# Splitting the first weight sum, its high part and its low part into halves where two seven-product units meet

## What is computed

```python
x = x + 0.5 * swiglu(rmsnorm(x, ffn1_norm[i]), ffn1_w_gu[i], ffn1_w_down[i])
...
x = x + m
x = x + 0.5 * swiglu(rmsnorm(x, ffn2_norm[i]), ffn2_w_gu[i], ffn2_w_down[i])
...
def swiglu(x, w_gu, w_down):
    gate, up = jnp.split(x @ w_gu, 2, axis=-1)
    return (jax.nn.silu(gate) * up) @ w_down
```

## Time and profile before

| what | value |
|---|---|
| median of 3 runs | 2016.92 us (2016.15 to 2017.0) |
| the profiled execution | 2016.95 us |
| its span | 2015.2 us |
| mean granted TensorE clock | 0.999 of full speed |
| TensorE busy | 1987.3 us, 99% |
| VectorE busy | 1680.8 us, 83% |
| ScalarE busy | 1242.4 us, 62% |

### The profile page before, as it was taken

How to read it: one execution, slowest core, us unless ns; L and a number is a source line. 1 busy time by engine, 2 the same in 40 slices (tenths; PEclk the granted TensorE clock), 3 DMA queues, 4 the chain that set the end, 5 groups by cost and what they waited for, 6 DMA issues and landing times.

```text
span 2015.2 us, 25299 instructions
## 1 busy us (share of the span) xinstructions
PE 1987.3 (99%) x10203; PEld 1684.0 (84%) x10203; DVE 1680.8 (83%) x1569; ACT 1242.4 (62%) x1317; POOL 189.3 (9%) x181
## 2 busy tenths in 40 slices
PE   7999999999999999999999999999999999999998
PEld 6888998888888889988888878988888888998877
DVE  7997568997999789969987997779988997568996
ACT  6565576665666566646665665446665665576664
POOL 2000001010000014411001010001001000001010
PEclk9999999999999999999999999999999999999999
DMA  9896535996897484368995996758986896535992
GB/s 278 274 268 214 181 105 141 277 258 222 231 270 230 146 271 131 126 230 222 277 272 162 277 253 191 209 186 232 286 257 175 268 267 216 176 105 144 275 261 103
DMA packets 250632, 436.65 MB, mean 217 GB/s; under 512 B 10924, under 2 KB 93188, under 8 KB 250004
## 3 DMA queue, kind: packets, MB, share of 16 engines
q1 hardware_dynamic: 215732, 363.34, 53.1%
q0 software_dynamic: 34496, 71.39, 19.7%
q10 hardware_dynamic: 288, 0.31, 0.0%
HBM read 433.92 MB, written 1.08 MB: 216 GB/s over the span
## 4 chain that ended last, share of the span: by engine, by line
PE 72%; DVE 14%; ACT 7%; issue 4%; DMA 2%; DVEq 0%; ACTq 0%; SPq 0%; POOLq 0%; POOL 0%
PE bank L1620 36%; PE bank L1761 23%; PE bank L1626 7%; DVE w_lo L1126 6%; ACT w_hi L744 6%; PE bank L1795 2%; DVE stage L1264 2%; DVE arena L1487 2%; DVE arena L1264 1%; DMA arena<-in_ffn_w_gu 1%; PE bank L1653 1%; PE bank L1935 1%; PE bank L1966 1%; PE bank L1948 0%; DMA stage<-in_ssd_w_in 0%
## 5 line engine op out<-in xcount | busy, mean ns | idle before, releaser
L1126 DVE TENSOR_TENSOR w_lo<-stage,w_hi 128x2048 fp32r<-128x2048 f32 (+1 forms) x245 | 562.3, 2298 | 85.1 <-ACT w_hi L744 82.5
L744 ACT ACTIVATE w_hi<-stage 128x2048 fp32r<-128x2048 f32 (+1 forms) x245 | 463.0, 1893 | 220.6 <-PE bank L1620 109.8
L1126 DVE TENSOR_TENSOR w_lo<-arena,w_hi 128x2048 fp32r<-128x2048 f32 (+1 forms) x199 | 450.3, 2267 | 81.6 <-ACT w_hi L744 80.0
L744 ACT ACTIVATE w_hi<-arena 128x2048 fp32r<-128x2048 f32 (+1 forms) x199 | 376.7, 1897 | 184.8 <-PE bank L1620 87.3
L1620 PE MATMUL bank<-w_hi,mt_hi 128*128 128x512 f32 x928 | 366.5, 395 | 0.4 <-DVE mt_lo L1373 0.4
L1620 PE MATMUL bank<-w_lo,mt_hi 128*128 128x512 f32 x928 | 361.4, 389 | 0.0
L1620 PE MATMUL bank<-w_hi,mt_lo 128*128 128x512 f32 x928 | 360.8, 390 | 0.0
L1761 PE MATMUL bank<-w_hi,mt_hi 128*128 128x512 f32 x512 | 205.2, 401 | 7.9 <-DVE w_lo L1126 7.8
L1620 PEld LDWEIGHTS bank<-w_hi,mt_lo 128*128 128x128 f32 x928 | 174.2, 188 | 36.9
L1626 PE MATMUL bank<-xt_hi,w_hi 128*128 128x256 f32 x704 | 203.4, 290 | 1.6 <-DVE arena L1487 1.1
L1620 PEld LDWEIGHTS bank<-w_hi,mt_hi 128*128 128x128 f32 x928 | 174.3, 188 | 35.4 <-DVE mt_lo L1373 0.8
(11 more groups left out here) (219 smaller groups left out, 2957.3 us busy)
## 6 DMA issues: line engine op xcount, KB each, us to landing
arena<-in_ffn_w_gu SPq DMA_DIRECT2D x82, 1024.0 KB, 5.9
stage<-in_ffn_w_gu SPq DMA_DIRECT2D x78, 1024.0 KB, 5.3
stage<-in_ffn_w_down SPq DMA_DIRECT2D x100, 512.0 KB, 5.0
arena<-in_ffn_w_down SPq DMA_DIRECT2D x76, 512.0 KB, 5.5
arena<-in_ffn_w_gu POOLq DMA_DIRECT2D x35, 1024.0 KB, 9.0
stage<-in_ffn_w_gu POOLq DMA_DIRECT2D x29, 1024.0 KB, 10.1
arena<-in_ffn_w_gu SPq DMA_DIRECT2D x20, 512.0 KB, 6.9
arena<-in_sb_w_qkv SPq DMA_DIRECT2D x16, 512.0 KB, 4.7
```

Of the source, the lines that this page charges most:

```text
L744: act.activation(w_hi[q][:, 0:c], stage[s][:, 0:c], ACT.Copy).then_inc(hi_done, 1)
L1126: dve.tensor_tensor(w_lo[q][:, 0:c], stage[s][:, 0:c], w_hi[q][:, 0:c].bitcast(F32), ALU.subtract).then_inc(lo_done, 1)
```

## The change

At the 24 places where two S units meet, the sum for A1, its high part and its low part are each done in two halves of 1024 columns (`HALF`), with new semaphores `sum_half`, `hi_half` and `lo_half`. On VectorE the low part's two halves now follow right behind the sum's, and `second_gate` comes behind them. TensorE's A1 waits for the first half before its first matmul and for the whole block before its seventh. The sum takes one more wait, for the low part of B11, whose block it overwrites.

```diff
--- before.py
+++ after.py
@@ -98,6 +98,12 @@
     return order + waiting + [(u, f"D{j}") for j in range(down_parts(u))], turned
 
 
+def junctions_to(f, u):
+
+    return f * sum(adjacent(v) for v in range(len(UNITS))) + sum(adjacent(v) for v in range(u + 1))
+
+
+HALF = (slice(0, 1024), slice(1024, 2048))
 FFN_ORDER, TURNED_AFTER = ffn_order()
 N_UNITS, N_SUMS = len(UNITS), UNITS.count("S")
 HOME = {"A1": "B11", "A2": "B11", "A3": "B12", "A4": "B21"}
@@ -429,6 +435,7 @@
         row_done = sem("row_done")
         xn_done, xn_act, xn_gained = sem("xn_done"), sem("xn_act"), sem("xn_gained")
         first_hi, first_lo = sem("first_hi"), sem("first_lo")
+        sum_half, hi_half, lo_half = sem("sum_half"), sem("hi_half"), sem("lo_half")
         xt_ps = sem("xt_ps")
         xg_done = sem("xg_done")
         xt_hi_done = sem("xt_hi_done")
@@ -731,6 +738,13 @@
                 p = max(r for r in range(n_phases) if base[r] <= n)
                 u, name = FFN_ORDER[n - base[p]] if PHASES[p][0] == "ffn" else (0, None)
                 sums = sums_before(nth("ffn", p), u)
+                if name == "A1" and adjacent(u):
+                    act.wait_ge(block_used, n - SPLIT_SLOTS + 1)
+                    act.wait_ge(sum_half, junctions_to(nth("ffn", p), u))
+                    act.activation(w_hi[q][:, HALF[0]], stage[s][:, HALF[0]], ACT.Copy).then_inc(hi_half, 1)
+                    act.wait_ge(w_summed, len(SUM_STEP) * sums + SUM_STEP[name])
+                    act.activation(w_hi[q][:, HALF[1]], stage[s][:, HALF[1]], ACT.Copy).then_inc(hi_done, 1)
+                    return
                 if name in SUM_STEP:
                     act.wait_ge(w_summed, len(SUM_STEP) * sums + SUM_STEP[name])
                 elif name == "A2":
@@ -1263,6 +1277,26 @@
                         to, a, b = w("B21"), w("B21"), w("B11")
                     dve.tensor_tensor(to, a, b, ALU.add).then_inc(w_summed, 1)
 
+                def weight_sum_by_halves(u):
+
+                    w = lambda b: stage[home[p, u, b][0]]
+                    dve.wait_ge(lo_done, b0 + FFN_ORDER.index((u, "B11")) + 1)
+                    dve.wait_ge(stage_in[home[p, u, "B12"][0]], home[p, u, "B12"][1])
+                    dve.tensor_tensor(w("B11")[:, HALF[0]], w("B12")[:, HALF[0]], w("B11")[:, HALF[0]],
+                                      ALU.add).then_inc(sum_half, 1)
+                    dve.tensor_tensor(w("B11")[:, HALF[1]], w("B12")[:, HALF[1]], w("B11")[:, HALF[1]],
+                                      ALU.add).then_inc(w_summed, 1)
+
+                def split_by_halves(u, n):
+
+                    s, q = slot_of[n], n % SPLIT_SLOTS
+                    dve.wait_ge(hi_half, junctions_to(f, u))
+                    dve.tensor_tensor(w_lo[q][:, HALF[0]], stage[s][:, HALF[0]], w_hi[q][:, HALF[0]].bitcast(F32),
+                                      ALU.subtract).then_inc(lo_half, 1)
+                    dve.wait_ge(hi_done, n + 1)
+                    dve.tensor_tensor(w_lo[q][:, HALF[1]], stage[s][:, HALF[1]], w_hi[q][:, HALF[1]].bitcast(F32),
+                                      ALU.subtract).then_inc(lo_done, 1)
+
                 def x_sums():
                     for i, (a, b, op) in enumerate(((xg[:, 1, :], xg[:, 3, :], ALU.subtract),
                                                     (x_sum[:, 0, :], xg[:, 0, :], ALU.subtract),
@@ -1319,12 +1353,15 @@
                         released(*FFN_ORDER[i - 1], i - 1)
                     if i == 1 and N_SUMS:
                         x_sums()
-                    if i + 2 <= len(FFN_ORDER) and (i == 0 or FFN_ORDER[i - 1] != (N_UNITS - 1, "A2")):
+                    if i + 2 < len(FFN_ORDER) and FFN_ORDER[i + 2][1] == "A1" and adjacent(FFN_ORDER[i + 2][0]):
+                        pass
+                    elif i + 2 <= len(FFN_ORDER) and (i == 0 or FFN_ORDER[i - 1] != (N_UNITS - 1, "A2")):
                         split(b0 + i + 2)
                     if i + 1 < len(FFN_ORDER):
                         u, name = FFN_ORDER[i + 1]
                         if name == "B11" and adjacent(u):
-                            weight_sum(u, "A1")
+                            weight_sum_by_halves(u)
+                            split_by_halves(u, b0 + i + 3)
                             second_gate(u - 1)
                         elif i >= 1 and FFN_ORDER[i - 1][1] == "A4" and adjacent(FFN_ORDER[i - 1][0] + 1):
                             hidden_summed(FFN_ORDER[i - 1][0], 1)
@@ -1753,9 +1790,11 @@
                                               start=kh == 0 and k == 0, stop=kh == 1 and k == 3)
                     mm.then_inc(block_used, 1)
 
-                def product(n, out_, x_, start, stop):
+                def product(n, out_, x_, start, stop, whole_from=None):
 
                     for k in range(4):
+                        if k == whole_from:
+                            block_in(n)
                         x, w = x_(k), w_pair(n, 512 * k, 512)
                         for a, b in PASSES:
                             mm = pe.matmul(out_[:, :], x[a], w[b], start=start and k == 0 and (a, b) == (0, 0),
@@ -1798,7 +1837,9 @@
 
                 for i, (u, name) in enumerate(FFN_ORDER):
                     n = b0 + i
-                    if n > 0:
+                    if name == "A1" and adjacent(u):
+                        pe.wait_ge(lo_half, junctions_to(f, u))
+                    elif n > 0:
                         block_in(n)
                     if n == 0:
                         opening_block()
@@ -1820,7 +1861,7 @@
                         product(n, bank[4], x_part(0, 0), True, True)
                     elif name == "A1":
                         pe.wait_ge(xs_lo_done, 4 * (f + 1))
-                        product(n, bank[5], x_sum_part(0), True, True)
+                        product(n, bank[5], x_sum_part(0), True, True, 2 if adjacent(u) else None)
                     elif name == "B22":
                         pe.wait_ge(part_copied, 3 * sums_before(f, u) + 2)
                         product(n, bank[5], x_sum_part(3), False, True)
```

## The result

| | before | after |
|---|---|---|
| median | 2016.96 us (4 runs, 2016.15 to 2017.28) | 2030.46 us (4 runs, 2030.39 to 2030.61) |
| ratio | | 1.0066, 95% interval 1.0054 to 1.0079 |
| span of the profiled run | 2015.2 us | 2028.6 us |
| mean granted clock | 0.999 | 1.0 |

The change makes the kernel slower by 13.5 us, 0.66%. Slower was forecast, with 2024.7 us; the time lies 1 us above the range, which ended at 2029.5.

What follows compares the result with a forecast made beforehand. TensorE, 99% busy, was taken as the bound, gaining or losing only by holes in its matmul stream. B22 starting 0.32 to 0.33 us later at 24 junctions adds 7.8 to 2016.9: 2024.7 us, range 2020 to 2029.5.

Steps and rivals of the forecast that it cites:

- The hole before A1: TensorE's wait for A1's low part at 24 junctions: 0.49 us each, forecast to go, with 1.44 to spare.
- a larger hole: TensorE before B22: forecast wait of about 0.9 us, with the start at 108.85 instead of a possible 107.93.
- the lateness of B22: TensorE's B22 at each junction: forecast to start at 108.85 against 108.53, 0.32 us later.
- the four halves: VectorE, two sum and two low-part halves at 1.13 each plus some waiting: 4.59 us before the second partial sum.
- not a third hole, but near one: TensorE's first down block after B22: its low part forecast in time by less than 0.1 us, so no wait.
- The hidden low part: VectorE's low part for the first down block: first bank forecast done at 111.51, block due to start at 111.65.
- such a restart at A1: TensorE's first matmul after the wait ahead of A1: 0.11 us extra, counted in the 0.60 per junction.
- the case of two holes: Rival: the down block's low part is late too, or halves cost 1.22; shift 0.5 to 0.7, 2029 to 2033, chance 0.13.
- TensorE's finer waits: TensorE's separate waits for A1's first half and, ahead of the seventh matmul, the second: costed at nothing.
- The earlier start of A2's load: POOL queue's second accumulating load, released by A1's low part: goes out 1.9 us earlier, costed at nothing.
- the hole that simply goes: Rival: ScalarE's lateness is swallowed, each junction gains 0.60, 14.4 us in all, 2002.5 us; chance 0.08.
- the 0.60: TensorE at A1, per junction: 0.49 us of waiting plus 0.11 for the first matmul after; 14.4 us over 24.

## Why the prediction was right and wrong

**Right: the mechanism.** The hole before A1 goes (0.49 in the row, 0 after), the second partial sum slips to 4.69 after the sum (4.59 forecast), the SiLU to 5.41 (5.30), B22's high part to 6.51 (6.39), the copy of A1's product to 10.12 (9.99), and a larger hole opens before B22, ended by that copy. Two runs show that this chain is the cause, each by one move: with the partial sum earlier, or the SiLU further back, the loss turns into a gain. The move without the halves has the same loss in large, and the copy moved out of the queue gives back its own length.

**Wrong: the size, 0.56 per junction instead of 0.32 to 0.33.** Two terms of the sum were too small.

The first is the lateness of B22. From A1's start to B22's I had 4.62; it measured 4.74, which is 24 times 0.12, 2.9 us. The step that was mis-sized is the one of the four halves: 4.69 from the sum to the second partial sum, where the sum had 4.59. From there to B22's start the way is as forecast, 6.15 (104.13 to 110.28, against 102.70 to 108.85), and A1's start lies 6.12 behind the sum's, as forecast. Within the halves it went wrong where ScalarE stands between them: the sum's first half took 0.09 to reach ScalarE (100.66 to 100.75), where I had taken 0.03 from a row with a whole block, so the low part started 2.41 after the sum instead of 2.33; the rest is a half that follows at 1.14, not 1.13. The mean over the junctions adds 0.02 to this one's 4.72.

The second is the step that I called "not a third hole, but near one". The hidden low part was forecast in time by less than 0.1 (my own figures, 111.51 and 111.65, are 0.14 apart), with nothing charged for the way to TensorE. Its first bank was ready at 112.99, and TensorE started the down block at 113.13; the distance is 0.15 at all 24 junctions, so the margin was used up. Undisturbed it would have started at 112.88 + 0.23 = 113.11. That delay is nearly nothing, but the first matmul after it took 0.31 to the next instead of 0.23. I had charged such a restart at A1 in the row before (0.11), and forgot it here: 0.02 and 0.08 at 24 places are 2.4 us. Forecast 7.8, plus 2.9 and 2.4, makes 13.1 of the 13.4 us by which the span grew.

The range took its upper end from the case of two holes, a rival that I put at 2029 to 2033 with a chance of 0.13. This is where the time fell: both holes, but with halves at 1.14 rather than at their full 1.22.

**What was costed at nothing.** TensorE's finer waits: nothing, as shown by their own run. The earlier start of A2's load: nothing in the changed kernel. But my rival of the hole that simply goes, 2002.5 us, was worked out with the same silence on the loads, and there it was wrong: at the junctions the 0.60 was had, and about half of it was lost again behind them, because loads that were hardly waited for at the old pace were waited for at the new one. I had looked at the issue times of the loads and not at how late they land.

**Breaking up instructions.** The Trainium skill (Perfetto Trace Analysis, Optimizing Scalar/DVE Operations) says that breaking up instructions on engines that cause bubbles may let work finish sooner. The run with the halves alone bears it out, by 7.3 us. In the changed kernel the finished work was not the work that was needed next.

## What to carry to other kernels

When work on one engine is moved ahead, look at what it is moved past, who reads that, and above all what else stands in the reader's in-order queue: 0.68 us of work that came 2.5 later cost 0.5 at each of 24 places, only because four instructions for someone else stood behind its reader. Count the slack of each consumer before and after: the gain of the first hole shortens the slack of the second by the same amount. And when an experiment gains half of the hole's worth, look for the transfer that was hidden until then; cutting it in half in both kernels tells quickly whether it is the one.

## What was not expected of the hardware

The distance from the end of one engine's instruction to the start of the one that waits for it on another engine differs from place to place, and hardly at all from junction to junction. From VectorE to ScalarE it was 0.03 for a whole block before the change and 0.09 for the sum's first half (at all junctions but the first). To TensorE it was 0.06 from A1's low part before the change, 0.14 to 0.15 from the copy of A1's product, and 0.15 from the hidden low part in the changed kernel. Each is small; on a chain with several such steps at 24 places they were a part of the miss.

A stop of TensorE costs more than its length. The first matmul of the down block started 0.00 to 0.05 late at the 24 junctions of the changed kernel, and at each of them the next one followed after 0.31 instead of 0.23. In the kernel with whole blocks in the new order, with a hole of 2.1 us at each junction, the granted clock fell to its lower level for about 3 us at 7 of the 24; in the changed kernel, with holes of about 1 us, it stayed at full speed. Why at these 7 and not at the others stays open.
